# Weaving the latent and the differential sample mixers of a hybrid encoder into one stage

## The reference

```
z = rmsnorm(x) @ w_in                    # columns split among four head groups
x += [ mla(z_a) | diff(z_b) | sgu(z_c) | gdn(z_d) ] @ w_out
x += convffn(rmsnorm(x))                 # gated MLP with a causal conv, d_ff 2816

# latent attention (mla): keys and values are expansions of a 128-wide latent
lat_all = concat([past_lat, lat]); k = [lat_all @ w_uk, kr_all]; v = lat_all @ w_uv
o = softmax(mask(q k^T * scale)) @ v     # 4 heads; the samples see 256 + 16 positions

# differential attention (diff): two softmaxes per head
p = softmax(mask(q k^T * scale + t5_bias)); w = p[:, 0] - lam * p[:, 1]
o = rmsnorm(w @ v_all, sub_g, eps=1e-5) * (1 - lam_init)

# gated delta rule (gdn)
y = silu(causal_dwconv(xqkv)); q, k, v = split(y)
q = l2norm(q) * dk ** -0.5; k = l2norm(k)
o, S = gated_delta(q, k, v, g, beta, S0)
o = rmsnorm(o, gdn_g) * silu(xg)
```

## Time and profile before

| | |
|---|---|
| time, median of 3 runs | 4477.47 us (4470.8 to 4479.23) |
| the profiled execution | 4470.32 us, span 4468.4 us |
| PE matmul busy | 3880.6 us, 87% of the span |
| DVE / ACT / POOL busy | 43% / 26% / 18% |
| mean granted TensorE clock | 0.898 of full speed |
| DMA | 15.7% of 16 engines, 51 GB/s |

### The profile page before, as it was taken

The page is one execution under the profiler, slowest core; times in us unless marked ns, Lnnn a source line. Parts: engine busy times, 40 slices in busy tenths (PEclk is TensorE's granted clock), DMA queues, the critical chain, the costliest instruction groups (busy, mean ns, idle before and its releaser), DMA issues. The chain is left out here.

```text
span 4468.4 us, 52346 instructions
## 1 busy us (share of the span) xinstructions
PE 3880.6 (87%) x21530; PEld 3464.1 (78%) x21530; DVE 1939.5 (43%) x3099; ACT 1146.7 (26%) x2101; POOL 819.5 (18%) x686
## 2 busy tenths in 40 slices
PE   3887899889779999999878879897988799999996
PEld 2865586569679999999866657864987799999995
DVE  3355243255434444454445634332543445444454
ACT  2244123333122221212133421232321321221211
POOL 2111010011122232222122100100112222222220
PEclk8999598789789999999989977985988899999998
DMA  4511111010101111111062210201001011111111
GB/s 152 160 59 59 48 59 69 22 48 1 31 24 41 43 38 43 38 38 43 21 184 85 75 58 30 77 36 69 1 6 39 27 43 38 39 42 35 46 38 46
DMA packets 102912, 229.80 MB, mean 51 GB/s; under 512 B 29156, under 2 KB 64484, under 8 KB 99016
## 3 DMA queue, kind: packets, MB, share of 16 engines
q1 hardware_dynamic: 102664, 226.36, 15.7%
HBM read 171.90 MB, written 52.07 MB: 50 GB/s over the span
## 5 line engine op out<-in xcount | busy, mean ns | idle before, releaser
L244 PE MATMUL PS<-h_split,w_split 128*128 128x384 f32 x3072 | 1069.7, 348 | 100.9 <-PEq L183 100.9
L246 PE MATMUL PS<-h_split,w_split 128*128 128x384 f32 x3072 | 1050.8, 342 | 0.0
L245 PE MATMUL PS<-h_split,w_split 128*128 128x384 f32 x3072 | 1047.5, 341 | 0.0
L239 POOL TENSOR_TENSOR w_split<-w_full,w_split 128x1024 fp32r<-128x1024 f32 (+1 forms) x196 | 494.3, 2523 | 1367.2 <-ACT w_split L231 1365.1
L244 PEld LDWEIGHTS PS<-h_split,w_split 128*128 128x128 f32 x3072 | 593.5, 193 | 116.7 <-issue 114.6
L245 PEld LDWEIGHTS PS<-h_split,w_split 128*128 128x128 f32 x3072 | 588.1, 191 | 1.5 <-issue 0.5
L246 PEld LDWEIGHTS PS<-h_split,w_split 128*128 128x128 f32 x3072 | 587.2, 191 | 0.0
L231 ACT CAST w_split<-w_full 128x1024 fp32r<-128x1024 f32 (+1 forms) x196 | 204.4, 1054 | 905.6 <-PE PS L246 763.6
L244 PE MATMUL PS<-ffn_act,w_split 128*128 128x384 f32 x1056 | 369.6, 350 | 71.7 <-DVE x L2035 54.4
L2035 DVE TENSOR_TENSOR x<-x,PS 128x384 f32<-128x384 f32 x528 | 287.1, 552 | 240.2 <-PE PS L246 240.0
L245 PE MATMUL PS<-ffn_act,w_split 128*128 128x384 f32 x1056 | 366.9, 347 | 0.0
(11 more groups left out here) (337 smaller groups left out, 5947.4 us busy)
## 6 DMA issues: line engine op xcount, KB each, us to landing
w_full<-in_w_up SPq DMA_DIRECT2D x88, 512.0 KB, 3.5
w_full<-in_w_down SPq DMA_DIRECT2D x44, 512.0 KB, 3.5
w_full<-in_w_in SPq DMA_DIRECT2D x40, 512.0 KB, 3.7
kq_keep<-split_rows SPq DMA_DIRECT2D x128, 128.0 KB, 2.4
kq_row<-kq_keep SPq DMA_DIRECT2D x32, 512.0 KB, 4.4
x_keep<-x SPq DMA_DIRECT2D x2, 4608.0 KB, 19.0
x<-x_keep SPq DMA_DIRECT2D x2, 4608.0 KB, 14.1
w_full<-in_w_out SPq DMA_DIRECT2D x16, 512.0 KB, 3.5
```

Source lines behind the costliest of these rows:

```text
L239: pool.tensor_tensor(ws[:, n % SSLOTS, 1, 0:w], wf[:, n % WSLOTS, 0:w], ws[:, n % SSLOTS, 0, 0:w].bitcast(F32), ALU.subtract).then_inc(w_l ...
L244: pe.matmul(out, w_hi, a_hi, start=first, stop=False)
L245: pe.matmul(out, w_hi, a_lo, start=False, stop=False)
L246: return pe.matmul(out, w_lo, a_hi, start=False, stop=last)
```

## The change

- `diff_samples_stage` and `mla_samples_stage` are replaced by `samples_stage`, which stands where the latter stood. Each engine's list is written by two generators, `latent()` and `diff()`, which hand over at fixed points; `weave` takes two steps of latent, and then one step of latent after every second step of diff. The rounds themselves are the same instructions. PSUM: the differential scores keep banks 0 and 1, the latent ones take 5 and 6; the combination has one bank (2) instead of two, and the latent transposes one (3) instead of two, each with a wait for the copy that empties it (`wd`, `ptd`).
- All caches, the samples' new keys and values (from the outputs in DRAM) and the bias are read during the latent prompt attention, into tiles of their own.
- The head norm of the differential output stands behind the new stage.
- `y` is read back at the start of the new stage, the gate in `gdn_mix_stage` behind `x`.
- SiLU is taken out of the sample stage: the head norm of `y` (`silu=True`) does it for tiles 0 to 3 ahead of its squares, each waiting for the one before, and for tiles 4 and 5 behind its last root; the head norm with the gate does the two gate tiles between the squares of block 1 and the first root.
- `y`, the gate and the tiles of `gdn_mix_stage` and `out_stage` have new addresses.

```diff
-        def head_norm_stage(src, tiles, div, eps, scale_of, base=8, gate=None, prepare=None):
+        def head_norm_stage(src, tiles, div, eps, scale_of, base=8, gate=None, prepare=None, silu=False):
...
+                        if gate is not None and b == 1:
+                            for n in range(tiles):
+                                act.activation(gate[:, n, :], gate[:, n, :], ACT.Silu).then_inc(silu_done, 1)
...
+                    if silu:
+                        for n in range(tiles):
+                            act.activation(src[:, n, :], src[:, n, :], ACT.Silu).then_inc(silu_done, 1)
+                            act.wait_ge(silu_done, n + 1)
                     walk(squares, root)
+                    if silu:
+                        for n in range(tiles, 6):
+                            act.activation(src[:, n, :], src[:, n, :], ACT.Silu)
...
+                def weave(latent, diff):
+                    next(latent)
+                    next(latent)
+                    for n in range(DEC_BATCH * 3 + 2):
+                        next(diff)
+                        if n % 2 == 1:
+                            next(latent)
...
+                @block.sync
+                def _(sp):
+                    sp.dma_start(y[:, :, :], y_keep).then_inc(y_moved, 16)
+                    sp.wait_ge(y_moved, 16)
...
-            diff_samples_stage(l, bias_s)
-            head_norm_stage(d_out, 2, HD, 1e-5, lambda n: G("sub_g"), base=24,
...
                     sp.dma_start(o_diff[:, :, :], d_out[:, :, :]).then_inc(kept_out, 16)
-                    sp.dma_start(y[:, :, :], y_keep).then_inc(y_moved, 16)
-                    sp.dma_start(gate_b[:, :, :], gate_keep).then_inc(y_moved, 16)
+                    sp.dma_start(cache_lT[:, :, :], d["c_latT"][l]).then_inc(caches, 16)
+                    sp.dma_start(cache_l[:, :, :, :], d["c_lat"][l]).then_inc(caches, 16)
+                    sp.dma_start(cache_dk[:, :, :, :], d["c_dkT"][l]).then_inc(caches, 16)
+                    sp.dma_start(cache_dv[:, :, :, :], d["c_dv"][l]).then_inc(caches, 16)
+                    sp.dma_start(k_s[:, :, :], d["o_dk"][l][:, :, SM]).then_inc(caches, 16)
+                    sp.dma_start(v_s[:, :], d["o_dv"][l][:, TT - 1, :]).then_inc(caches, 16)
+                    sp.dma_start(bias_back[:, :], d["bias_s"]).then_inc(caches, 16)
                     sp.wait_ge(kept_out, 32)
+                    sp.dma_start(cache_kr[64:96, :, :], d["c_krT"][l]).then_inc(caches, 16)
+                    sp.wait_ge(caches, 128)
...
-            mla_samples_stage(l, kT, val, lat_s)
-            head_norm_stage(y, 4, 1.0, 1e-6, lambda n: HD ** -0.5 if n < 2 else 1.0)
+            samples_stage(l, lat_s)
+            head_norm_stage(o_diff, 2, HD, 1e-5, lambda n: G("sub_g"), base=24,
...
+            head_norm_stage(y, 4, 1.0, 1e-6, lambda n: HD ** -0.5 if n < 2 else 1.0, base=24, silu=True)
```

More of the change, by code:

```diff
@@ L139, in build @@
         dqT = at("dqT", [P, 2, TOK], R(0))
+        d_out = dqT
         dkT = at("dkT", [P, 2, TOK], R(2))
@@ L1421, in gdn_mix_stage @@
[L1421 to L1429, removed]
@@ L2135, in _, with latent @@
+                    weave(latent(), diff())
                 @block.scalar
                 def _(act):
[L2137 to L2150 removed]
+                    def latent():
+                        yield True
+                        yield True
+                        for u in range(4):
+                            act.wait_ge(mmx, u + 1)
+                            if u >= 2:
+                                act.wait_ge(ptr, u - 1)
+                            act.activation(mP[:, u % 2, :], PS[:, 5 + u % 2, 0:384], ACT.Exp, bias=mstat[:, 0, u:u + 1],
+                                           accum_out=mstat[:, 1, u:u + 1]).then_inc(mpd, 1)
+                            yield True
+                            act.wait_ge(ptr, u + 1)
+                            if u >= 2:
+                                act.wait_ge(mav, u - 1)
+                            act.copy(mPT[:, u % 2, :], PS[:, 3, 0:384]).then_inc(ptd, 1)
+                            yield True
+                            yield True
+                        yield True
@@ new lines, in diff @@
+                    def diff():
+                        yield True
+                        for b in range(DEC_BATCH):
+                            act.wait_ge(dmx, b + 1)
+                            if b >= 2:
+                                act.wait_ge(wr, b - 1)
+                            act.activation(dP[:, b % 2, :], PS[:, b % 2, 0:384], ACT.Exp, bias=dstat[:, 0, b:b + 1],
+                                           accum_out=dstat[:, 1, b:b + 1]).then_inc(dpd, 1)
+                            yield True
+                            act.wait_ge(wr, b + 1)
+                            if b >= 2:
+                                act.wait_ge(dav, b - 1)
+                            act.copy(WT[:, b % 2, :, :].rearrange("p a c -> p (a c)"), PS[:, 2, 0:192]).then_inc(wd, 1)
+                            yield True
+                            yield True
+                        yield True
@@ L2365, in build @@
             stat = at("mla_stat", [P, 3, PT_TILES * HEADS, 1], R(17.6))
-            with stage(*ATT_SEMS) as (block, sems):
+            with stage(*ATT_SEMS, "caches") as (block, (*sems, caches)):
                 @block.sync
```

416 lines of the change are left out of this document (213 added, 203 removed).

## The result

The changed kernel takes 4436.3 us (median of 4, 4433.1 to 4437.9), the kernel before 4475.4 us beside it; the ratio is 0.9909, 95% interval 0.9893 to 0.9925. That is 39 us faster, and the forecast was 33. The profiled execution went from 4470.3 to 4433.1 us, its span from 4468.4 to 4431.1.

The account below looks back on a forecast made before the run. PE's own instructions at 1.2 GHz were taken to bound both sample stages. Per layer -139.8 + 117 + 6.1 + 0.1 = -16.6 us, twice -33, from the 4477.5 us median to 4444 us; range 4403 to 4463.

Parts of the forecast that it names:

- The cache waits: Sample stages: PE's waits for caches, about 13 and 8.2 us, 21 us a layer, go with loads issued during the attention.
- Rounds at the lower clock: Woven stage: PE's rounds stay at 1.2 GHz, eight differential 67.4 us and four latent 43.7; 122.5 with waits and no burst.
- Two bursts, 5.5 us: Woven stage: two short rises to 2.4 GHz a layer take 5.5 us off 122.5, giving 117 us.
- Waits: PE in the woven stage: start 1.9 us, first differential scores 2.4, before values four of 0.4, end 5.5 with hand-overs.
- SiLU: Moved out of the sample stage, it costs 6.1 us in `y`'s head norm and 0.1 in the gated one, per layer.
- the gate's read: Delta-rule stage: the gate's read joins that of `x` ahead of the sample states; priced at nothing, 2 us at most.
- The drain: ACT table switches: the skill's 1.38 us extra each would cost 4 us a layer; left out of the forecast.
- Clock elsewhere: Other stages: stretches of lower clock come at other moments once stages shift, worth 10 us either way.
- Rival A: Clock stays up in the woven stage: 4354 us all the way, 4404 half the time; chance 0.14, 0.05 all the way.
- the clock up all the time: Woven stage at 2.4 GHz throughout: PE work of 112 us becomes 63, 72 us with the same waits.
- Rival C: Slower: the woven lists wait for each other, stage 157 us, 23 us a layer lost, 4524 us; chance 0.04.
- Rival B: Little gained: no burst, hand-overs cost 5 us, clock elsewhere takes 5 a layer; 4475 us, halfway 4460; chance 0.13.

Follow-up runs that it names:

- experiment 1: Changed kernel with every engine running the whole differential list first, then the latent list, caches still read during the attention: 4448.8 us, ratio 0.9939.
- experiment 2: Changed kernel with the caches read at the start of the woven stage, latent keys first, each group with its own wait: 4444.8 us, ratio 0.9934.
- experiment 7: Changed kernel with both parts undone: lists one behind the other, caches read at the stage's start, differential keys first: 4472.4 us, ratio 0.9993.
- experiment 10: Kernel before with its mask matmuls over all 128 rows of their tables, no weaving or early reads: 4433.4 us, ratio 0.9905.
- experiment 4: Changed kernel with the six SiLU of `y` moved from its head norm into ACT's gap in the woven stage: 4421.1 us, ratio 0.9891.
- experiment 5: Changed kernel with the woven stage's mask matmuls taking all 128 rows of their tables instead of 8: 4356.9 us, ratio 0.9738.
- experiment 3: Changed kernel with DVE's eight diagonal-query products ahead of the first latent maximum instead of behind it: 4438.5 us, ratio 0.9917.

## Why the prediction was right

**The cache waits.** Right: all 21 us are gone, and no load stands in PE's waits. That it was the early read which removed them is only part of it; experiments 1, 2 and 7 show that either part removes most. The 12.3 us of the earlier trace rows was not of a load alone, as I read it: the 2 MB of keys are issued ahead of it and land in 8.0 us, so both together took little more than 12. The error was on the safe side.

**Rounds at the lower clock: the mis-sized term.** With no burst the stage was to take 122.5 us; it took 117.7 in layer 0. A period was to be 2 x 8.42 + 10.92 + 0.41 = 28.17 us, and is 26.89; four of them make 5.1 us. The rows show it: where a latent set follows a differential one, the last 8-row mask and the first 32-row matmul start together (782.46, 782.47), so that the set takes 3.57 us and not 4.18; and a combination costs 1.34 us to the next matmul (772.36 to 773.70), its 1.54 being a duration that overlaps what follows. The remaining 0.47 us are the same kind of thing in the values and transposes, 0.81 us from start to start for a duration of 0.90. I mixed durations and distances. That the overlap at the mask depends on its rows is seen in experiment 10, where it goes when the mask has 128.

**Two bursts, 5.5 us: wrong in layer 0, near in layer 1.** None came in layer 0; one of 6.8 us in layer 1 gave 5.3. In layer 0 the error of the bursts and that of the rounds cancel by luck: 117 us was forecast, and 117.7 came. In layer 1, where the bursts were right, the stage took 112.3. Why one layer has a burst and the other none stays open.

**Waits.** 2.4 us before the first differential scores: 2.3. Four of 0.4: four, 1.6 in all. Start 1.9: a projection of 1.1 us and a wait of 0.8. End: 1.69 before the last combination for 1.9.

**SiLU.** 6.1 us in the head norm of `y`: 6.07. Gated one 0.1: 0.11 up to the root, but with the delta-rule stage in front it takes 0.9 and 0.8 us more, inside the 2 us allowed for the gate's read. Experiment 4 confirms that the whole move in the head norm of `y` lay on the path. The drain by which the Trainium skill (ScalarE: Activation LUTs, What ACT_TABLE_LOAD costs) would make each switch dearer is in no row here: SiLU starts 0.02 us behind its table.

**Clock elsewhere.** Within the 10 us allowed: the attention of layer 1 lost 4.1 us, the FFN stages won 1.9 and 3.7.

**Rival A** did not happen but was real: with full rows the clock is up for 46 of 74.3 us. That this is near the 72 us I had put for "the clock up all the time" is chance, for the sets also got shorter by overlap. What I had called against it, "32 or 8 rows in part", is what experiment 5 removed. The Trainium skill (TensorE: Matmul & The Clock Gate, Part 1) has activity release the throttle. Read plainly, this case's trace disagrees again: PE was busy for 29.59 of 30.00 us at a granted clock of 0.50. **Rival C**, waits between the lists: PE's waits sum to 9.3 us, 1.1 of them at the border; it was far off. **Rival B** needed hand-overs that cost, and there are none.

## What to carry to other kernels

When PE is busy and its clock low, look at the rows of what it streams: a matmul of a few rows between full ones cost twice here, in overlap and in clock, and filling it with zero rows won 79 us. It is to be measured each time, for the latent stage alone lost 1.2 us by it. Before loads are moved early, divide the waits and put the work on the smallest load first: in the woven list that left 4 us a layer of the 21, and dividing alone won 6 a layer in the old kernel. Work moved to where "nothing lies beside it" costs its full length, and the tail of a stage, behind its last exponential, took it for nothing.

## What the runs showed of the hardware

- Two matmul chains that write to different halves of the partitions overlapped where both had 128 rows throughout: 2.81 us for a set of differential scores (1.76 without the masks, a wait of 0.20 in it), against 4.17 with 8-row matmuls in it, at 1.2 GHz.
- An 8-row mask and a 32-row matmul behind it started 0.01 us apart; with 128 rows in the mask it was 0.56 us (experiment 10).
- The same number of matmuls and columns, with 128 rows instead of 8 in 24 of them, took the stage from 1.6 us at 2.4 GHz to 46; without these 24 it was 1.7 us. PE was busy for 93, 87 and 90% of the stage.
- A DVE wait of 2.3 us removed in one stage (experiment 3) was worth nothing in the median; a burst of the clock in layer 1 was gone in the same run.
